# Alternating wide and narrow matmuls in the projections, and another order of the attention work on VectorE and ScalarE

## The reference, cut to what matters

```
D_MODEL = 1024; SEQ = 256; D_FF = 2816; HEAD_DIM = 128; N_HEADS = 8

def short_conv_mixer(h, w_in, w_conv, w_out):
    bg, cg, xv = jnp.split(h @ w_in, 3, axis=-1)
    return (bg * causal_dwconv(cg * xv, w_conv)) @ w_out

def conv_ffn(h, w_up, w_conv, b_conv, w_down):
    g, u = jnp.split(h @ w_up, 2, axis=-1)
    g = causal_dwconv(g, w_conv) + b_conv
    return (silu(g) * u) @ w_down

# layer 0
x = x + short_conv_mixer(rmsnorm(x, norm_mix[0]), ...)
x = x + conv_ffn(rmsnorm(x, norm_ffn[0]), ...)
k, v = split(rmsnorm(x, kv_norm) @ w_kv, 2)          # shared keys and values, 8 heads of 128
# layer 1
q = rmsnorm(x, norm_mix[1]) @ b_w_q
p = softmax(q k^T * 128**-0.5 - slope[head] * distance, causal)   # one block of 256 keys
x = x + (p v) @ b_w_o
x = x + conv_ffn(rmsnorm(x, norm_ffn[1]), ...)
return rmsnorm(x, final_norm)
```

## Time and profile before

| what | value |
|---|---|
| median of three executions | 587.86 us |
| profiled execution: time, span of its instructions | 587.91 us, 586.1 us |
| TensorE matmul busy | 578.0 us, 99% |
| TensorE weight load busy | 499.4 us, 85% |
| VectorE busy | 420.2 us, 72% |
| ScalarE busy | 315.1 us, 54% |
| mean granted TensorE clock | 0.997 of full |

### The profile page before, as it was taken

The page is one execution under the profiler, slowest core; times in us unless marked ns, Lnnn a source line. Parts: engine busy times, 40 slices in busy tenths (PEclk is TensorE's granted clock), DMA queues, the critical chain, the costliest instruction groups (busy, mean ns, idle before and its releaser), DMA issues.

```text
span 586.1 us, 8105 instructions
## 1 busy us (share of the span) xinstructions
PE 578.0 (99%) x3119; PEld 499.4 (85%) x3119; DVE 420.2 (72%) x508; ACT 315.1 (54%) x380; POOL 10.2 (2%) x22
## 2 busy tenths in 40 slices
PE   8999999999999999999999999999999999999995
PEld 6988888888888888888888899888888888888884
DVE  4688877768667667766886788896786667667765
ACT  5544553567544554555545666645665544554541
POOL 2000000000000000000100000000000000000001
PEclk9999999999999999999999999999999999999998
DMA  9995667456655665556654644275545655664001
GB/s 289 344 308 170 216 216 239 140 177 207 216 187 175 214 197 165 193 171 209 215 180 148 247 144 143 74 256 167 177 160 211 216 195 169 212 200 159 1 0 73
DMA packets 80917, 108.08 MB, mean 184 GB/s; under 512 B 1833, under 2 KB 71665, under 8 KB 80882
## 3 DMA queue, kind: packets, MB, share of 16 engines
q1 hardware_dynamic: 80160, 104.97, 54.2%
q10 hardware_dynamic: 722, 2.63, 1.3%
HBM read 106.54 MB, written 1.05 MB: 184 GB/s over the span
## 4 chain that ended last, share of the span: by engine, by line
PE 95%; DVE 2%; ACT 1%; issue 1%; POOL 0%; DVEq 0%; ACTq 0%; POOLq 0%
PE pair L948 36%; PE pair L953 19%; PE acc L994 7%; PE acc L996 7%; PE acc L998 7%; PE pair L932 3%; PE pair L933 3%; PE pair L934 3%; PE pair L1008 2%; PE acc L934 1%; PE acc L933 1%; PE acc L932 1%; PE acc L1114 1%; DVE wgt L617 1%; PE acc L1119 1%
## 5 line engine op out<-in xcount | busy, mean ns | idle before, releaser
L617 DVE TENSOR_TENSOR wgt<-raw,wgt 128x2048 fp32r<-128x2048 f32 x94 | 214.7, 2290 | 53.5 <-ACT wgt L359 53.2
L948 PE MATMUL pair<-hA,wgt 128*128 128x512 f32 x864 | 207.2, 391 | 0.0
L359 ACT ACTIVATE wgt<-raw 128x2048 fp32r<-128x2048 f32 x94 | 179.5, 1912 | 24.7 <-PE acc L998 21.2
L948 PEld LDWEIGHTS pair<-hA,wgt 128*128 128x128 f32 x864 | 159.4, 188 | 31.4
L953 PEld LDWEIGHTS pair<-hA,wgt 128*128 128x128 f32 x864 | 111.3, 191 | 4.6
L953 PE MATMUL pair<-hA,wgt 128*128 128x256 f32 x864 | 112.7, 283 | 0.0
L994 PE MATMUL acc<-wgt,kq_hi 128*128 128x512 f32 x160 | 49.5, 391 | 0.0
L996 PE MATMUL acc<-wgt,kq_hi 128*128 128x512 f32 x160 | 49.4, 390 | 0.0
L998 PE MATMUL acc<-wgt,kq_lo 128*128 128x512 f32 x160 | 49.3, 389 | 0.0
L427 ACT ACTIVATE scratch<-scratch 128x512 f32<-128x512 f32 x22 | 13.9, 632 | 59.8 <-DVE scratch L695 59.8
L441 ACT ACTIVATE scratch<-pair 128x512 f32<-128x512 f32 x20 | 11.9, 595 | 58.3 <-PE pair L953 58.3
(11 more groups left out here) (143 smaller groups left out, 584.2 us busy)
## 6 DMA issues: line engine op xcount, KB each, us to landing
raw<-in_ffn_w_up SPq DMA_DIRECT2D x44, 1024.0 KB, 5.1
raw<-in_ffn_w_down SPq DMA_DIRECT2D x22, 1024.0 KB, 4.9
raw<-in_a_w_in SPq DMA_DIRECT2D x11, 1024.0 KB, 10.7
raw<-in_w_kv SPq DMA_DIRECT2D x8, 1024.0 KB, 5.2
raw<-in_a_w_out SPq DMA_DIRECT2D x4, 1024.0 KB, 4.8
raw<-in_b_w_q SPq DMA_DIRECT2D x4, 1024.0 KB, 5.8
raw<-in_b_w_o SPq DMA_DIRECT2D x4, 1024.0 KB, 5.7
raw<-in_a_w_in SPq DMA_DIRECT2D x2, 512.0 KB, 6.9
```

Source lines behind the costliest of these rows:

```text
L359: act.activation(split_slot(s)[0], raw[:, s % RAW, :], ACT.Copy).then_inc(w_hi_ready, 2 if s + 1 in AHEAD else 1)
L617: dve.tensor_tensor(wlo, raw[:, s % RAW, :], whi.bitcast(F32), ALU.subtract).then_inc(w_lo_ready, 2 if s + 1 in AHEAD else 1)
L948: pe.matmul(pair[b][:, e, :].rearrange("p (a n) -> p a n", a=2), whi[:, w], hid[:, :, k, :], start=k == 0, stop=False)
```

## The change

There are two parts. In `project`, the tuple of halves is gone: the function takes one half e, and for each chunk k it issues the 512-wide matmul and right after it the 256-wide one, with the same products and the same number of instructions. Callers that want both halves call it twice. In the attention loop, VectorE's and ScalarE's lists are put in another order. No instruction is added or taken away on any engine.

```
-            def project(s, b, hid, halves):
+            def project(s, b, hid, e):
                 whi, wlo = split_slot(s)
-                for e in halves:
-                    for k in range(KD):
-                        w = slice(256 * k + P * e, 256 * k + P * e + P)
-                        pe.matmul(pair[b][:, e, :]..., whi[:, w], hid[:, :, k, :], start=k == 0, stop=False)
-                for e in halves:
-                    for k in range(KD):
-                        w = slice(256 * k + P * e, 256 * k + P * e + P)
-                        last = pe.matmul(pair[b][:, e, 0:S], wlo[:, w], hid[:, 0, k, :], start=False, stop=k == KD - 1)
+                dst = pair[b][:, e, :]
+                for k in range(KD):
+                    w = slice(256 * k + P * e, 256 * k + P * e + P)
+                    pe.matmul(dst..., whi[:, w], hid[:, :, k, :], start=k == 0, stop=False)
+                    last = pe.matmul(dst[:, 0:S], wlo[:, w], hid[:, 0, k, :], start=False, stop=k == KD - 1)

 # ScalarE
             for p in range(NH // 2 - 1):
                 kq_copy(2 * p + 2)
-                hi(KQ0 + 2 * p + 5)
-                exp(2 * p)
-                exp(2 * p + 1)
                 kq(2 * p + 2)
                 if p:
                     heads_mixed(p - 1)
+                exp(2 * p)
+                exp(2 * p + 1)
+                hi(KQ0 + 2 * p + 5)
                 kq_copy(2 * p + 3)
                 kq(2 * p + 3)
                 heads_probs(p)
-                hi(KQ0 + 2 * p + 6)
+                if p < NH // 2 - 2:
+                    hi(KQ0 + 2 * p + 6)
+            hi(O0 + 2)
             heads_mixed(NH // 2 - 2)

 # VectorE
             for p in range(NH // 2 - 1):
-                row_max(2 * p)
-                row_max(2 * p + 1)
                 kq_whole(2 * p + 2)
-                normal_probs(2 * p)
-                normal_probs(2 * p + 1)
                 kq(2 * p + 2)
                 if p:
                     heads_mixed(p - 1)
+                row_max(2 * p)
+                row_max(2 * p + 1)
+                normal_probs(2 * p)
+                normal_probs(2 * p + 1)
+                lo(KQ0 + 2 * p + 5)
                 kq_whole(2 * p + 3)
                 kq(2 * p + 3)
                 heads_probs(p)
-                lo(KQ0 + 2 * p + 5)
                 if p < NH // 2 - 2:
                     lo(KQ0 + 2 * p + 6)
-            heads_mixed(NH // 2 - 2)
             row_max(NH - 2)
             row_max(NH - 1)
+            heads_mixed(NH // 2 - 2)
             normal_probs(NH - 2)
             normal_probs(NH - 1)
             lo(O0 + 2)
+            lo_ahead(2)
             heads_probs(NH // 2 - 1)
             lo(O0 + 3)
             heads_mixed(NH // 2 - 1)
-            lo_ahead(2)
             lo(FFN[1])
```

More of the change, by code:

```diff
@@ L940, in wait_slot @@
                 pe.wait_ge(w_lo_ready, after(s + 1, turn, TURN))
-            def project(s, b, hid, halves):
+            def project(s, b, hid, e):
                 whi, wlo = split_slot(s)
-                for e in halves:
-                    for k in range(KD):
-                        w = slice(256 * k + P * e, 256 * k + P * e + P)
-                        pe.matmul(pair[b][:, e, :].rearrange("p (a n) -> p a n", a=2), whi[:, w], hid[:, :, k, :],
-                                  start=k == 0, stop=False)
-                for e in halves:
-                    for k in range(KD):
-                        w = slice(256 * k + P * e, 256 * k + P * e + P)
-                        last = pe.matmul(pair[b][:, e, 0:S], wlo[:, w], hid[:, 0, k, :], start=False, stop=k == KD - 1)
+                dst = pair[b][:, e, :]
+                for k in range(KD):
+                    w = slice(256 * k + P * e, 256 * k + P * e + P)
+                    pe.matmul(dst.rearrange("p (a n) -> p a n", a=2), whi[:, w], hid[:, :, k, :], start=k == 0, stop=False)
+                    last = pe.matmul(dst[:, 0:S], wlo[:, w], hid[:, 0, k, :], start=False, stop=k == KD - 1)
                 return last
@@ L1061, in two_after_opening @@
                 turn_opening(o, 0)
-                project(s, 0, hA, (0,))
+                project(s, 0, hA, 0)
                 turn_opening(o, 1)
-                project(s, 0, hA, (1,)).then_inc(slot_done, 1)
+                project(s, 0, hA, 1).then_inc(slot_done, 1)
                 wide_slot(s + 1, 1, hA)
@@ L1068, in wide_slot @@
                 wait_slot(s, turn)
-                project(s, b, hid, (0, 1)).then_inc(slot_done, 1)
+                for e in range(2):
+                    last = project(s, b, hid, e)
+                last.then_inc(slot_done, 1)
             def deep_slot(s, left, first=False, turn=None):
@@ L1136, in _ @@
             pe.wait_ge(opening_copied, 1)
-            project(A_IN + 2, 0, hA, (0,))
+            project(A_IN + 2, 0, hA, 0)
             pe.wait_ge(par_ready, 3)
@@ L1140, in _ @@
             turn_opening(0, 1)
-            project(A_IN + 2, 0, hA, (1,)).then_inc(slot_done, 1)
+            project(A_IN + 2, 0, hA, 1).then_inc(slot_done, 1)
             wide_slot(A_IN + 3, 1, hA)
@@ L1170, in _ @@
             pe.wait_ge(v_lo_ready, 3)
-            project(KQ0, 0, hA, (0,))
+            project(KQ0, 0, hA, 0)
             pe.wait_ge(h_lo_ready, step4(3, 1, 1))
-            project(KQ0, 0, hA, (1,)).then_inc(slot_done, 1)
+            project(KQ0, 0, hA, 1).then_inc(slot_done, 1)
             pe.wait_ge(v_lo_ready, 4)
@@ L1208, in _ @@
                 pe.wait_ge(kq_sum, 2 * p + 1)
-                project(sK, 0, hA, (0, 1)).then_inc(slot_done, 1)
+                for e in range(2):
+                    last = project(sK, 0, hA, e)
+                last.then_inc(slot_done, 1)
                 if p:
```

## The result

The changed kernel takes 598.19 us (median of 5 executions, 596.52 to 599.29) against 587.86 us before. The ratio is 1.0174, with a 95% interval of 1.0154 to 1.0195. That is 10.3 us slower. The forecast was slower by 4.9 us, so the direction was right and the size was half. The profiled execution took 597.63 us, with a span of 595.7 us against 586.1.

The account below looks back on a forecast made before the run. The prediction took TensorE's row of matmuls as the bound, with VectorE's longer round becoming it in the attention: 587.9 + 6.3 (waits) - 0.4 (boundary) - 1.0 (alternation) = 592.8 us, range 589.4 to 599.4.

Parts of the forecast that it names:

- Part 2, the waits: Attention: VectorE's reordered round grows to 16.58 us against TensorE's 14.59, so TensorE ends 6.3 us late at `scores(6)`.
- The boundary: Behind the attention: VectorE work done earlier lets the residual and first transposes start sooner, -0.4 us.
- Part 1, the pair distance: Projections: one 512-wide and one 256-wide matmul in turn cost 347 ns, saving 1.0 us in all.
- the steady cost is the same, and only the passages go: Projections: alternation keeps 347 ns a pair, removing only slow wide-narrow transitions; a feed-forward unit takes 16.53 instead of 16.58 us.
- alternation hurts: Projections: a slow wide matmul at every pair, about 353 ns, +4.3 us instead of -1.0; 598.1 us, chance 0.20.
- The clock: Attention: TensorE's clock may drop in the new two-microsecond waits, costing 3 us more; 595.8 us, chance 0.05.
- The rival that loads hide fully: Projections: weight loads are covered at every pair, below about 341 ns, -7.0 us; 586.8 us, chance 0.07.

Follow-up runs that it names:

- part 2 alone: Only the attention lists of VectorE and ScalarE reordered, `project` as in the kernel before: 595.11 us, ratio 1.0122.
- part 1 alone: Only `project` and its callers changed to alternate wide and narrow matmuls, attention lists as in the kernel before: 590.90 us, ratio 1.0043.
- groups of two: Kernel before with `project` issuing two wide matmuls, then two narrow ones, attention lists unchanged: 588.35 us, ratio 0.9999.

## Why the prediction was wrong, by its own steps

**Part 2, the waits: right.** The round of 16.58 us was 16.56. Waits of 2.0, 2.0 and 2.3 us were forecast, and nothing or 0.1 us in round 0. The steps measured between starts are 1.9, 2.0 and 2.2, and 0.2 in round 0. The boundary gave back 0.4, by starts, as forecast. The term was 5.9 us, and the trace of part 2 alone has 6.1.

**Part 1, the pair distance: mis-sized, with the wrong sign.** The term was -1.0 us, and it measured +3.0 by the traces. The step that failed is "the steady cost is the same, and only the passages go", 347 ns at every pair. The sum of the two steady distances is right in the mixer and for the projections ahead of the attention (5.54 us a slot). It is wrong in the 16 feed-forward units that follow a down slot, which take 16.79 us instead of 16.53. (The prediction counted 18 such units. In each layer the unit j = 2 follows other projections and not a down slot, and keeps 347 ns.) That these 16 are entered from a run of 24 wide matmuls decides it: an extra run like that turned the mixer to 353 ns, and four small matmuls turned the feed-forward units to 347. The first rival, *alternation hurts*, had named 353 ns, but everywhere, at 0.16 us a unit where 0.21 was measured, and had 598.1 us for it. It was wrong about where, and that it lies so near to the measured 598.19 us is luck: its +4.3 us for part 1 stand against a measured +3.0, and the clock made up the difference.

**The clock: a rival that came on top.** The prediction gave it 0.05 and treated it as an alternative. It is no alternative to the waits but rides on them. In 4 of the 7 executions of the first measurement, and then in 3 of 5, the mean granted clock was 0.996 or less. Only one of these executions has a trace, and it shows the fall; for the others the fall is inferred from the mean clock and the time. The other three executions of the first measurement average 597.0 us. So 598.19 is some 9.1 us of both parts (5.9 or 6.1, and 3.0) and, reckoned by that sorting, 1.2 us of the clock in the median.

**The sum.** Had part 1 been +3.0, the forecast would have been 596.8 us, which the undisturbed executions meet (596.5 to 597.6).

**The rival that loads hide fully** wanted a pair under about 341 ns, and no pattern here is shorter than 347 ns. The prediction had put beside it what the Trainium skill ("TensorE: Matmul & The Clock Gate", section "Back-to-back issue gap") says of weight loads being pipelined. No trace here shows that bringing a pair under 347 ns. The shortest distance behind a narrow matmul's start, 112 ns, is paid back at the next wide one (231 to 233 ns instead of 227).

**What stays open.** What the two patterns are in the engine. Another place in PSUM, fewer or more changes of width, and another order at the start of the run do not explain them. Behind a full-paced run of 512 or 256 columns every entry brought the long one. Behind 128-wide matmuls five entries in the trace of the changed kernel have the short one and three the long one. Among these are the two key projections shown above, and they differ in the same way, 353 and 347 ns, with part 1 alone, where no wait is ahead of either. So the widths of the matmuls ahead do not decide it there, and what does is not shown. It may be a matter of how far TensorE's instructions are ahead, but no run here looked at that. Why the clock falls in some executions with the same waits, and not in others, is open too.

No version beat the kernel before. The traces leave some 0.2 us for alternation in the mixer alone and 0.4 at the boundary, both below what can be told apart.

## What to carry to other kernels

Walk the lists of the engines that are not the bound, with their waits for one another, and compare the round with that of the bound: 12.3 us of work in a round of 14.6 hid a dependent chain of 16.6. A distance between matmuls read from unmixed runs is not good for a mixture; with 900 pairs 6 ns are worth 5 us, so measure the mixture where it is entered as in the kernel. And when a change opens waits of a microsecond or two on TensorE, add a term for the clock to the waits themselves.

## What the runs showed of the hardware that was not expected

- The same alternating instructions run at 347 or 353 ns a pair. The pattern is chosen at the entry and then kept for more than thirty microseconds (six slots of the mixer, 353 ns throughout). A run of 24 matmuls of 512 columns ahead brought 353 ns in all 16 feed-forward units, and four matmuls of 128 columns in between brought 347 ns in all 16.
- Eight changes of width in a slot cost no more than one (348 ns a pair in groups of two, 588.35 us), though the single change shows five slow matmuls behind it (234, 236, 228, 232 and 231 ns in the trace of the kernel before, where 227 is steady).
- TensorE's clock can fall to its lower level 1.4 us behind a single wait of 1.7 us. By the matmuls it stays there from 373.7 to 377.2 us. It need not fall: of the two traces of the changed kernel, whose waits are the same, one has a fall at that place and the other a granted clock of 1.00 in every stretch from 345 to 400 us.
